# Three of four channel blocks of a depthwise convolution go from VectorE to GpSimd in a one-core decoder layer

## The reference, cut to what matters

```python
def conv_branch(u, dw, dw_b, ln_g, ln_b, pw, pw_b):
    a, b = jnp.split(u, 2, axis=-1)
    glu = a * jax.nn.sigmoid(b)                       # 512 tokens x 512 channels
    y = causal_depthwise_conv(glu, dw, width=31) + dw_b
    yn = layer_norm(y) * ln_g + ln_b                  # over the 512 channels
    return silu(yn) @ pw + pw_b
```

```python
sa = einsum('hvk,hk->hv', state, -kk_t)
state = state * w_t + sa * (kk_t * a_t) + v_t * k_t
y_t = einsum('hvk,hk->hv', state, r_t)
```

## Time and profile before

| | |
|---|---|
| median of 3 runs | 2345.38 us |
| the profiled execution's own time | 2345.38 us |
| span of that execution | 2343.6 us |
| TensorE busy in the span | 2219.4 us, 95% |
| VectorE busy | 1518.5 us, 65% |
| GpSimd busy | 384.0 us, 16% |
| stretch from the first finished block of glu to the end of the recurrence | 115.8 to 438.3 us |
| VectorE taps, L1195 | 120 instructions, 168.7 to 454.8 us |

### The profile page before, as it was taken

One profiled execution on the slowest core, in us unless ns is written; L12 is line 12 of the kernel. 1 busy time (PEld: TensorE's weight loads), 2 busy tenths in 40 slices (PEclk: granted clock), 3 DMA queues, 4 the chain that ended last, 5 costly groups with the idle time before them and its releaser, 6 DMA issues.

```text
span 2343.6 us, 33776 instructions
## 1 busy us (share of the span) xinstructions
PE 2219.4 (95%) x11162; PEld 1855.1 (79%) x11162; DVE 1518.5 (65%) x3026; ACT 792.4 (34%) x1088; POOL 384.0 (16%) x451
## 2 busy tenths in 40 slices
PE   6998898689979999899998999999999999999997
PEld 4887888568768788788887888888888888888885
DVE  5479889874469999576674554555545555455555
ACT  4222111322232222466665333333333333333332
POOL 0000000220000244699994000000000000000000
PEclk9998888899989999999999999999999999999998
DMA  4210000022222344355556544344443444444431
GB/s 150 97 46 1 1 1 1 19 97 93 89 80 73 113 140 143 135 215 206 192 197 228 167 156 139 124 154 152 155 134 128 157 148 153 135 132 155 149 106 38
DMA packets 153920, 281.09 MB, mean 120 GB/s; under 512 B 9824, under 2 KB 75488, under 8 KB 151296
## 3 DMA queue, kind: packets, MB, share of 16 engines
q1 hardware_dynamic: 153568, 277.10, 35.4%
q0 software_dynamic: 288, 3.15, 0.4%
HBM read 227.78 MB, written 52.43 MB: 120 GB/s over the span
## 4 chain that ended last, share of the span: by engine, by line
PE 85%; DVE 7%; issue 6%; DMA 1%; ACT 1%; POOL 0%; SPq 0%; DVEq 0%; POOLq 0%; ACTq 0%
PE bank L305 85%; DVE cy L1195 2%; PE bank L374 1%; DVE gdev L1396 0%; DVE be L1244 0%; DMA wlo<-wlora 0%; DMA gl<-g_dram 0%; DVE nt L1291 0%; DVE nt L1293 0%; DVE nn L1284 0%; DVE wL L1125 0%; DVE xx L1281 0%; DMA g_dram<-ge 0%; DVE lt L1288 0%; DVE h L1151 0%
## 5 line engine op out<-in xcount | busy, mean ns | idle before, releaser
L305 PE MATMUL bank<-h2H,uH 128*128 128x512 f32 x1024 | 412.5, 403 | 2.2 <-POOL uL L1654 2.2
L305 PE MATMUL bank<-aH,vH 128*128 128x512 f32 x1024 | 399.2, 390 | 9.8 <-DVE vL L1564 9.8
L305 PE MATMUL bank<-h2H,uL 128*128 128x512 f32 x1024 | 400.8, 391 | 0.0
L305 PE MATMUL bank<-h2L,uH 128*128 128x512 f32 x1024 | 399.8, 390 | 0.0
L305 PE MATMUL bank<-aL,vH 128*128 128x512 f32 x1024 | 399.1, 390 | 0.0
L305 PE MATMUL bank<-aH,vL 128*128 128x512 f32 x1024 | 398.9, 390 | 0.0
L1564 DVE TENSOR_TENSOR vL<-vraw,vH 128x512 fp32r<-128x512 f32 x256 | 176.1, 689 | 235.9 <-ACT vH L763 235.9
L763 ACT ACTIVATE vH<-vraw 128x512 fp32r<-128x512 f32 x256 | 161.0, 630 | 414.3 <-PE bank L305 414.3
L1673 POOL TENSOR_SCALAR oh<-cst,e2s 128x128 f32<-128x128 f32 x384 | 266.1, 711 | 17.1 <-PE bank L305 12.4
L305 PEld LDWEIGHTS bank<-aH,vH 128*128 128x128 f32 x1024 | 192.7, 188 | 50.3 <-DVE vL L1564 10.2
L305 PEld LDWEIGHTS bank<-h2H,uL 128*128 128x128 f32 x1024 | 192.9, 188 | 41.9
(11 more groups left out here) (260 smaller groups left out, 3271.0 us busy)
## 6 DMA issues: line engine op xcount, KB each, us to landing
uraw<-uT SPq DMA_DIRECT2D x128, 512.0 KB, 4.2
vraw<-v_tab SPq DMA_DIRECT2D x256, 256.0 KB, 2.7
wraw<-wall SPq DMA_DIRECT2D x68, 512.0 KB, 3.5
w_dram<-wst SPq DMA_DIRECT2D x16, 2048.0 KB, 6.6
wg<-w_dram SPq DMA_DIRECT2D x32, 1024.0 KB, 6.5
g_dram<-ge SPq DMA_DIRECT2D x64, 256.0 KB, 2.2
gl<-g_dram SPq DMA_DIRECT2D x32, 512.0 KB, 7.8
xin<-xT SPq DMA_DIRECT2D x2, 1024.0 KB, 6.1
```

Of the source, the lines that this page charges most:

```text
L305: return pe.matmul(out, lhsT, rhs, start=start, stop=stop, skip_group_check=True)
```

## The change

The 31 taps of blocks 0, 1 and 2 are done by GpSimd, those of block 3 stay on VectorE. GpSimd does a tap in two instructions: a `tensor_tensor` that multiplies the shifted `glu` by a weight column spread over 512 elements into a new buffer `tapped` (two halves, used in turn), and a `tensor_tensor` that adds it to `cy`. A block's first tap is one `tensor_scalar`. Each addition waits for its multiplication. This stands at the start of GpSimd's queue, ahead of `hL`. On VectorE `taps(2)` is gone from the inversion's levels, and `taps(9)` has become `taps(4)`; four tiles have 32 places for the 31 taps of block 3. The completion of block 3 has a semaphore of its own, `conv_last`.

```diff
@@ tensor @@
             for i in range(CB):
-                pe.wait_ge(conv_out, i + 1)
+                if i < CB - 1:
+                    pe.wait_ge(conv_out, i + 1)
+                else:
+                    pe.wait_ge(conv_last, 1)
@@ vector @@
             def taps(k):
                 for _ in range(k):
-                    i, j = done_taps[0] // TAPS, done_taps[0] % TAPS
-                    if i == CB:
+                    i, j = CB - 1, done_taps[0]
+                    if j == TAPS:
                         return
                     done_taps[0] += 1
                     if j == 0:
-                        wait_taken(dve, f"w{W_CONV + 2 * i + 1}")
                         ins = tsc(cy[:, i, :], glu[:, i, 0:T], vc("dw", i * TAPS), vc("dwb", i), ALU.mult, ALU.add)
...
-                        ins.then_inc(conv_out, 1)
+                        ins.then_inc(conv_last, 1)
...
-                    taps(2)
                     for par in range(2):
                         for name, dst in ((f"N{lv}{par}_{t}", nn[:, par]), (f"NT{lv}{par}_{t}", nt[:, s, par])):
...
-                taps(9)
+                taps(4)
                 new_state(2 * t)
...
-                taps(9)
+                taps(4)
                 new_state(2 * t + 1)
-            taps(CB * TAPS)
+            taps(TAPS)
             split_l(W_MIX)
             split_l(W_MIX + 1)
 
-            dve.wait_ge(conv_out, CB)
+            dve.wait_ge(conv_out, CB - 1)
+            dve.wait_ge(conv_last, 1)
@@ gpsimd, at the start @@
+            pool.wait_ge(s_cst, 48)
+            pool.wait_ge(zero_ready, 1)
+            steps = 0
+            for i in range(CB - 1):
+                wait_taken(pool, f"w{W_CONV + 2 * i + 1}")
+                for j in range(TAPS):
+
+                    if j == 0:
+                        ins = pool.tensor_scalar(cy[:, i, :], glu[:, i, 0:T], vc("dw", i * TAPS), vc("dwb", i),
+                                                 ALU.mult, ALU.add)
+                    else:
+                        ins = pool.tensor_tensor(tapped[:, j % 2, :], glu[:, i, j:j + T],
+                                                 vc("dw", i * TAPS + j).broadcast_to([P, T]), ALU.mult)
+                    ins.then_inc(pool_order, 1)
+                    steps += 1
+                    if j:
+                        pool.wait_ge(pool_order, steps)
+                        ins = pool.tensor_tensor(cy[:, i, :], cy[:, i, :], tapped[:, j % 2, :], ALU.add)
+                        ins.then_inc(pool_order if j < TAPS - 1 else conv_out, 1)
+                        steps += j < TAPS - 1
```

More of the change, by code:

```diff
@@ L144, in build @@
     mv = at("mv", 189, [P, 512])
+    tapped = at("tapped", 195, [P, 2, T])
     sa = at("sa", 199, [P, 512])
@@ L248, in build @@
         lora_shifted, lora_ready = sem("lora_shifted"), sem("lora_ready")
-        conv_out, cy_sq = sem("conv_out"), sem("cy_sq")
+        conv_out, conv_last, cy_sq = sem("conv_out"), sem("conv_last"), sem("cy_sq")
         cy_part, o_high = sem("cy_part"), sem("o_high")
@@ L1645, in _ @@
             wait_taken(pool, f"ST{2 * TT - 1}")
-            pool.wait_ge(conv_out, CB)
+            pool.wait_ge(conv_out, CB - 1)
             pool.dma_start(x1[:, :, :], xT).then_inc(xr_loaded, 16)
@@ L1665, in _ @@
                 pool.tensor_copy(e2s[:, :], et[:, 1, bass.ds(2 * T_W * i, 2 * T_W)]).then_inc(pool_order, 1)
-                pool.wait_ge(pool_order, i + 1)
+                pool.wait_ge(pool_order, i + steps + 1)
                 for j in range(4):
```

## The result

| | before | after |
|---|---|---|
| median | 2345.66 us (4 runs) | 2374.57 us (4 runs, 2371.53 to 2375.89) |
| span of the profiled execution | 2343.6 us | 2372.8 us |
| TensorE busy | 2219.4 us | 2227.0 us |
| VectorE busy | 1518.5 us | 1536.5 us |
| GpSimd busy | 384.0 us | 619.8 us |

The ratio is 1.0121 (95% interval 1.0109 to 1.0134): slower by 28.9 us, where 19 had been forecast. All 15 executions of the changed kernel that were timed, the four of the table among them, lie between 2371.22 and 2377.76 us. The windows of the changed kernel, cut at the first product of each token tile and at the last new_state, answer to the earlier trace rows; columns as there.

The account below looks back on a forecast made before the run. TensorE was taken to bound the inversion's levels and VectorE the rest of a tile. Recurrence with projections +35 us and tail -16 gave +19 on 2345.4, so 2364.4 us, range 2334 to 2388.

Parts of the forecast that it names:

- the eight taps: VectorE taps in the old kernel's tail beside GpSimd's hL: about 1.65 us each against 0.76 alone.
- Price: VectorE's two-SBUF-operand instructions wait beside GpSimd: 0.89 us behind another payer, 0.3 behind one on PSUM; 21 us a tile.
- the idle 1.39 us: VectorE's wait in a token tile, in which what follows ld, scan, ex and kn of decays was to hide.
- Gain: Taps leaving VectorE in a tile: twice five at 0.785 us go, but only the first five count, 3.9 us.
- End of GpSimd's taps: GpSimd's 183 instructions at 1.5 us each take 275 us from 115.8 us, ending at 391 us.
- Projections: Stretch from 115.8 to 154.4 us, ahead of the glu products: +8 us, between 0 and +12.
- Tail: Behind the last new_state twelve taps are gone: -16 us, between -12 and -18.
- No contention: Rival: no contention worth the name between GpSimd and VectorE, -29 us, 2316 us; chance 0.08.
- half the price: Rival: GpSimd's spread column needs few reads, so turns are shorter, -11 us, 2334 us; chance 0.14.
- three quarters of it: Rival: VectorE pays three quarters of the forecast's contention cost, +4 us, 2349 us; chance 0.14.
- GpSimd as the bound: Rival: GpSimd's multiplications take 2.6 us, all four tiles pay, +36 us, 2381 us; chance 0.10.
- That PSUM instructions are shut out too: Rival: VectorE's PSUM instructions also wait and bound the levels, +17.5 us a tile, 2430 us; chance 0.04.

Follow-up runs that it names:

- relief: The changed kernel without GpSimd's 183 tap instructions, blocks 0 to 2 of the convolution being zeros: 2300.1 us.
- one_gated: GpSimd takes block 0 alone (61 instructions), dealt out over four tiles, each share starting with that tile's inversion levels; VectorE keeps blocks 1 to 3: 2331.49 us.
- one_free: GpSimd takes block 0 alone (61 instructions), in one go from the first finished block of glu; VectorE keeps blocks 1 to 3: 2349.34 us.
- merged: The changed kernel with a tile's eight small be and ke scalings made two instructions of 128x512: 2368.36 us.
- late: The changed kernel with GpSimd's 183 instructions starting only when the projections' features are written: 2361.44 us.

## Why the prediction was right, and where its terms were off

The forecast was slower, at 2364.4 us; the time is 2374.6, inside the range. The mechanism held: two-operand instructions at 1.5 to 1.75 us, those on a bank unchanged, levels at 23.0 us from their first sum to their last (22.5 before in tile 1, and 23.0 in relief, so that half a microsecond isn't GpSimd's), subtraction of the mean 3.7 us behind the last new_state, `conv_out` never waited for. relief and one_gated against one_free make it shown, and not only argued. One reading in the prediction goes too far: that the eight taps agree with a full wait for the other engine. They show that the two contend, but a tap paid 0.89 us beside a GpSimd instruction that takes 1.30. By its own steps:

- **Price, mis-sized.** The terms of the price add up to 8 + 2 x (12 + 3.9) + (4.5 + 3.9) = 48 us; the last new_state stands at 411.6 us in relief and at 485.35 in the changed kernel, 73.8 later. Three assumptions failed. Small instructions were priced at 0.45 us; `be` and `ke` paid 0.58 and 0.69 and `sqh` and `k` 0.9 each (1260 and 1228 ns in the mean, against 344 and 340), a full turn like the large ones, and merged gave 4.5 to 5.0 us a tile. `k` and the small copy `pend` (1158 ns against 162) have one input and were given no price: the prediction used the rule of the Trainium skill ("SBUF — State Buffer", section "Who interferes with whom") on two inputs and passed over the one there on copies and `tensor_scalar`. And what follows `decays` did not hide in the idle 1.39 us: VectorE came later than the bank that it had waited for. A discount of 0.85 was taken off on top. Of the instructions priced at 0.3, `kn` behind the reciprocal (739 ns) and the `nn` and `nt` of the masks that stand behind one on PSUM (865 and 785 ns against 692) came cheaper still, `sdec` behind `be` dearer (1.16 us against 0.68), and `bb`, priced in full at 0.89, took 720 ns, since it stands behind new_state, which reads PSUM.
- **Gain, mis-sized the other way.** "the second five taps free nothing: TensorE's own work from 289.33 to 304.73 stays" failed. That work ran at the lower level of the clock behind the wait of 4.78 us; in relief the wait is 1.35 us, the work runs at the upper level, VectorE becomes the bound, its second five taps count, and the half tile is 5 us shorter. The gain in the recurrence is 25.8 us, not 3 x 3.9 + 1.5 = 13.2. In the changed kernel it shows only in tile 2, since the wait in tiles 0 and 1 grew to 6.90 and 7.43 us and the granted clock stayed at 0.56 and 0.58; VectorE, busy 23.83 of the 24.10 us in that half of tile 1, sets its length. So the clock, for which the sum took nothing, counted on the side of the gain.
- **End of GpSimd's taps.** Forecast at 391 us, it came at 361.7, since the multiplication takes 1.04 to 1.08 us (1.3 taken): 1.34 us for each instruction in the mean. Tile 2 begins at 361.53 us, so it had the whole gain, -8.1 us, instead of a loss of 4.5. That the two times fall together is luck; without it the miss would have been some 12.6 us larger.
- **Projections.** +14.9 instead of +8. late shows that it is all GpSimd's (back at 39.3 us). The last three `glu` products came 5.5, 11.9 and 14.8 us later than before (133.20, 151.42 and 165.19 us), so the three stretches ahead of them cost 5.5, 6.4 and 2.9 where 1.5, 4.8 and 1.5 had been forecast. The first is the worst: its four small `k` took 4.76 us instead of 1.11.
- **Tail.** -16.4 for -16.
- **Rivals.** No contention (2316), half the price (2334) and three quarters of it (2349) fell with the four taps at 6.2 to 6.4 us, 1.55 to 1.6 each: three quarters of 0.89 on 0.76 would be 1.43. GpSimd as the bound fell with the 1.08 us multiplication. That PSUM instructions are shut out too fell with L1308.

So the price was 25.6 us too low and the gain in the recurrence 12.6 too low. Half of the one cancelled the other by luck: 13 us too little were left, less 0.4 in the tail and 2.4 behind it, which makes the 10 us between 19 and 28.9.

What stays open: the price of a two-input GpSimd instruction that falls on VectorE lies between 0.40 and 0.46 us in two kernels and near nothing in the levels. It is the kernel's lost time over their number, what TensorE's clock takes with it included, and no run shows how it depends on the order in which the two engines ask. Why a `tensor_scalar` with one operation takes twice what one with two does on GpSimd wasn't tried.

## What to carry to other kernels

Before elementwise work goes to an idle GpSimd, count the VectorE instructions that will stand beside it with operands in SBUF, small ones in full: each pays up to one turn whatever its size. The same work is nearly free where VectorE reads from PSUM, so place it there (17.9 us for one changed wait) and leave GpSimd few two-input instructions. Where a wait of TensorE is followed by work at half speed, price the clock with the wait, and measure gain and price apart, as relief does.

## What the runs showed of the hardware that was not expected

- On GpSimd a `tensor_tensor` whose second operand is a spread column takes 1.04 us, one with two full tensors 1.27.
- GpSimd's `tensor_scalar` of 128x512: 1566 ns with one operation, 773 with two, a copy 617.
- One-input GpSimd instructions cost the kernel 0.10 us each here, two-input ones 0.40 to 0.46 (time lost by the kernel over the number of GpSimd instructions).
- A VectorE copy of 128x8 takes 1.00 us beside two-input GpSimd work, 0.17 alone.
- Beside GpSimd's memsets, which only write, VectorE's one-input `tensor_scalar` of 128x512 takes 696 ns instead of 427, its two-input instructions what they take alone.
